# Output-projection halves inside the decode's closing chain, and running sums of squares on VectorE in two feed-forwards and the gate stage

## What is computed

```python
def rmsnorm(x, g):
    xf = x.astype(jnp.float32)
    y = xf * lax.rsqrt(jnp.mean(xf * xf, axis=-1, keepdims=True) + EPS)
    return (y * g.astype(jnp.float32)).astype(x.dtype)

def swiglu(x, w_gate, w_up, w_down):
    return (jax.nn.silu(x @ w_gate) * (x @ w_up)) @ w_down

x = x + FFN_RES * swiglu(rmsnorm(x, ffn_norm[layer, 0]), ...)   # ffn00, ffn10
# layer 0: s5_mixer, with   out = (y @ w_glu_v) * sigmoid(y @ w_glu_g)
# layer 1: mla_mixer, with  o = softmax(q . cache) . cache, mapped by w_uv;  return o @ w_o
x = x + FFN_RES * swiglu(rmsnorm(x, ffn_norm[layer, 1]), ...)   # ffn01, ffn11
```

## Time and profile before

| | us |
|---|---|
| median of 3 runs | 2287.75 |
| lowest and highest | 2266.84, 2288.28 |
| the profiled execution | 2266.89 |
| its span, first to last instruction | 2264.6 |
| closing chain, last scores ready to first projection matmul | 1785.27 to 1814.88 |

### The profile page before, as it was taken

The page is one execution under the profiler, slowest core; times in us unless marked ns, Lnnn a source line. Parts: engine busy times, 40 slices in busy tenths (PEclk is TensorE's granted clock), DMA queues, the critical chain, the costliest instruction groups (busy, mean ns, idle before and its releaser), DMA issues.

```text
span 2264.6 us, 46747 instructions
## 1 busy us (share of the span) xinstructions
PE 2127.8 (94%) x19825; PEld 2020.4 (89%) x19825; DVE 1087.0 (48%) x1563; ACT 745.5 (33%) x1080; POOL 157.2 (7%) x250
## 2 busy tenths in 40 slices
PE   7999999974899999999999999988888799999998
PEld 6999999953899999999999999975656599999998
DVE  5453676697344445322654442234763234544422
ACT  4222222543343343222422222242543124434211
POOL 3002010140000000000000000000027100000000
PEclk9999999997999999999999999999999799999999
DMA  6232323100222333332333333221237322333332
GB/s 134 84 107 71 93 85 107 39 3 6 85 84 85 93 93 88 103 90 63 95 92 93 93 101 90 79 80 29 50 105 203 88 66 78 90 93 93 105 90 77
DMA packets 355924, 192.56 MB, mean 85 GB/s; under 512 B 33005, under 2 KB 350443, under 8 KB 355795
## 3 DMA queue, kind: packets, MB, share of 16 engines
q1 hardware_dynamic: 348736, 180.19, 27.8%
q0 software_dynamic: 5488, 9.03, 1.4%
q10 hardware_dynamic: 1570, 1.48, 0.3%
HBM read 184.23 MB, written 3.02 MB: 83 GB/s over the span
## 4 chain that ended last, share of the span: by engine, by line
PE 85%; DVE 7%; ACT 3%; SPq 2%; issue 2%; DMA 1%; DVEq 0%; ACTq 0%
PE ps L1724 75%; PE ps L1737 2%; DVE stmp L466 2%; PE ps L2132 1%; PE ps L2257 1%; DVE xs L470 1%; PE ps L2288 1%; SPq L440 1%; SPq L438 1%; DVE stmp L469 1%; PE ps L2019 1%; PE ps L1743 1%; DVE wl L1126 1%; PE ps L2235 1%; DMA xin<-x_prompt 0%
## 5 line engine op out<-in xcount | busy, mean ns | idle before, releaser
L1724 PE MATMUL ps<-xh,wh 128*128 128x260 f32 x3296 | 870.1, 285 | 30.8 <-DVE xl L1441 15.8
L1724 PE MATMUL ps<-xl,wh 128*128 128x260 f32 x3296 | 863.6, 284 | 0.0
L1724 PE MATMUL ps<-xh,wl 128*128 128x260 f32 x3296 | 667.4, 284 | 0.0
L1724 PEld LDWEIGHTS ps<-xh,wh 128*128 128x128 f32 x3296 | 626.9, 190 | 37.7 <-issue 30.6
L1724 PEld LDWEIGHTS ps<-xl,wh 128*128 128x128 f32 x3296 | 625.0, 190 | 0.0
L1724 PEld LDWEIGHTS ps<-xh,wl 128*128 128x128 f32 x3296 | 512.1, 190 | 0.0
L650 ACT ACTIVATE wh<-raw 128x1024 fp32r<-128x1024 f32 (+1 forms) x150 | 175.6, 1170 | 597.7 <-PE ps L1724 596.5
L1126 DVE TENSOR_TENSOR wl<-raw,wh 128x1024 fp32r<-128x1024 f32 (+1 forms) x150 | 206.1, 1374 | 238.9 <-ACT wh L650 238.8
L1724 PE MATMUL ps<-hh,wh 128*128 128x260 f32 x1056 | 277.7, 284 | 0.0
L1724 PE MATMUL ps<-hl,wh 128*128 128x260 f32 x1056 | 275.6, 282 | 0.0
L668 ACT ACTIVATE wh<-raw 128x1024 fp32r<-128x1024 f32 (+1 forms) x124 | 135.3, 1091 | 418.3 <-PE ps L1724 418.3
(11 more groups left out here) (403 smaller groups left out, 2200.3 us busy)
## 6 DMA issues: line engine op xcount, KB each, us to landing
raw<-ffn_w_gate SPq DMA_DIRECT2D x88, 512.0 KB, 3.8
raw<-ffn_w_up SPq DMA_DIRECT2D x88, 512.0 KB, 3.8
raw<-ffn_w_down SPq DMA_DIRECT2D x64, 704.0 KB, 4.5
cb<-cache_ckv SPq DMA_DIRECT2D x72, 128.0 KB, 2.8
cb<-cache_ckv POOLq DMA_DIRECT2D x56, 128.0 KB, 2.9
raw<-s_w_glu_v SPq DMA_DIRECT2D x8, 512.0 KB, 3.8
raw<-s_w_glu_g SPq DMA_DIRECT2D x8, 512.0 KB, 3.7
raw<-mla_w_o SPq DMA_DIRECT2D x8, 512.0 KB, 4.1
```

What stands on the lines that cost most here:

```text
L1724: got = mm(ps[0:width, bank + half, 0:HALF], w[par_][:, k * width:k * width + width], src[:, k0 + k, half * HALF:half * HALF + HALF], star ...
```

## The change

First, the running sum. In ffn01, ffn10 and the gate stage VectorE adds the square of tile d-1 to the running sum in the other `sq` buffer (`add_squares`), from d = 2 on, and signals `ss_done` itself. TensorE sums only twice per stage: the running sum of tiles 0 to 6, and tile 7. The other stages keep their sums.

Second, the output projection. The first four tiles are made in halves of 24 matmuls (`wo_half`), the first 260 columns in banks 0 to 3, the others in banks 4 to 7. The first halves stand in the last iteration of the decode loop and between the steps of the closing chain. ScalarE and VectorE split two more weight blocks, WO0+2 and WO0+3, into extra buffers `w4h`, `w4l`, which lie where `cb0` was. The small results of the chain move to bank 7, two small VectorE steps (`own_w`, `own_s`) move to iteration 1 of the decode loop, and the turning of the maxima moves ahead of the last output. The update of x for these four tiles is two instructions.

```diff
+                w4h, w4l = take(m, ("w4h", [P, 2, KD * P], F32R), ("w4l", [P, 2, KD * P], F32R))
@@ ScalarE, decode loop
+                else:
+                    act.wait_ge(d_o, NB - 1)
+                    for j in range(2):
+                        act.wait_ge(w_in[(WO0 + j) % 2], slots.arrived(WO0 + 2 + j))
+                        run(w4h[:, j, :], raw[(WO0 + j) % 2][:, 0:KD * P], ACT.Copy).then_inc(w_hi, 1)
@@ ScalarE, projection
-                if d < KD - 1:
+                if d < 2:
+                    n = WO0 + 4 + d
+                    act.wait_ge(w_in[n % 2], slots.arrived(n))
+                    act.wait_ge(w_used, WO0 + d + 1)
+                    run(wh[n % 2][:, 0:KD * P], raw[n % 2][:, 0:KD * P], ACT.Copy).then_inc(w_hi, 1)
+                elif 4 <= d < KD - 1:
                     his(WO0 + d + 2)
@@ VectorE
+            def add_squares(tick):
+
+                now, before = tick % 2, (tick - 1) % 2
+                dve.wait_ge(sq_rdy, tick + 1)
+                tt(sq[:, now, :], sq[:, now, :], sq[:, before, :], ALU.add).then_inc(ss_done, 1)
@@ VectorE, ffn01 and ffn10
                     los(bd + 2 * d + 2)
+                    if name in NEXT and d >= 2:
+                        if d >= 3:
+                            dve.wait_ge(ss_done, SQ[name] + d - 2)
+                        add_squares(SQ[name] + d - 1)
                     update(d, bd + 2 * d + 1, d % 2)
@@ VectorE, gate stage
                 j = d % 2
+                if d >= 2:
+                    if d >= 3:
+                        dve.wait_ge(ss_done, SQ["glu"] + d - 2)
+                    add_squares(SQ["glu"] + d - 1)
                 if d < KD - 1:
                     los(g0 + 2 * d + 3)
@@ VectorE, decode loop and chain
+            def wide_lo(j):
+
+                dve.wait_ge(w_hi, WO0 + 3 + j)
+                tt(w4l[:, j, :], raw[(WO0 + j) % 2][:, 0:KD * P], w4h[:, j, :], ALU.subtract).then_inc(w_lo, 1)
+                else:
+                    wide_lo(0)
@@
-            copy(nwt[:, :, :], ps[:, 3, 0:NB * HP].rearrange("p (b h) -> p b h", b=NB))
             tt(wsel[:, :, :], cst[:, C_S32:C_S32 + HP].unsqueeze(1).to_broadcast([P, NB, HP]),
                ps[:, 4, 0:NB].unsqueeze(2).to_broadcast([P, NB, HP]), ALU.mult).then_inc(d_fin, 1)
+            own(copy(nwt[:, :, :], ps[:, 7, NB * HP:2 * NB * HP].rearrange("p (b h) -> p b h", b=NB)))
+            wide_lo(1)
@@ VectorE, projection
+                if d < 4:
+                    tt(x[:, d, 0:HALF], x[:, d, 0:HALF], ps[:, d, 0:HALF], ALU.add)
+                    tt(x[:, d, HALF:TOK], x[:, d, HALF:TOK], ps[:, d + 4, 0:HALF], ALU.add).then_inc(x_upd, 1)
@@ TensorE, ffn01 and ffn10, after the down-projection
+                if not each:
+                    pe.wait_ge(ss_done, S + KD - 2)
+                    sums(S + KD - 2, S % 2, True)
@@ TensorE, gate stage
                 product(g0 + 2 * d, g0 % 2, KD, X, 2 * (d % 2), ready=(xl_rdy, GEN["glu"]) if d == 0 else None)
+                if d == KD - 1:
+                    pe.wait_ge(ss_done, S + KD - 2)
+                    sums(S + KD - 2, S % 2, True)
                 if d >= 1:
-                    sums(S + d - 1, (S + d - 1) % 2, d == 1)
                     pe.wait_ge(g_sig, d)
                 product(g0 + 2 * d + 1, 1 - g0 % 2, KD, X, 5, free=d == KD - 1)
@@ TensorE, decode loop and chain
+            def wo_half(d, half, k0, k1):
+
+
+                pe.wait_ge(w_lo, WO0 + d + 1)
+                hi_, lo_ = (wh[(WO0 + d) % 2], wl[(WO0 + d) % 2]) if d < 2 else (w4h[:, d - 2], w4l[:, d - 2])
+                for k in range(k0, k1):
+                    for m, (w, srcs_) in enumerate(((hi_, (xh, xl)), (lo_, (xh,)))):
+                        for s, src in enumerate(srcs_):
+                            got = mm(ps[:, d + 4 * half, 0:HALF], w[:, k * P:k * P + P], src[:, k, half * HALF:half * HALF + HALF],
+                                     start=k == 0 and m == 0 and s == 0, stop=k == KD - 1 and m == 1)
+                if half == 1:
+                    got.then_inc(w_used, 1)
+                if b == NB - 1:
+                    pe.wait_ge(a_ol, NH // 2)
+                    wo_half(0, 0, 0, KD)
                 pe.wait_ge(d_e, b + 1)
@@
+                else:
+                    turn(ps[0:NB, 7, 0:P], mb[:, :])
+                    turn(ps[0:NB, 7, P:2 * P], lb[:, :]).then_inc(d_rt, 1)
+                    wo_half(1, 0, 0, 3)
@@ after the output of the last token
+            wo_half(1, 0, 3, KD)
+            wo_half(2, 0, 0, 3)
             pe.wait_ge(d_ws, 1)
...
+            wo_half(2, 0, 3, 5)
             pe.wait_ge(d_fin, 1)
...
+            wo_half(2, 0, 5, KD)
             pe.wait_ge(d_fin, 2)
...
+            wo_half(3, 0, 0, KD)
             pe.wait_ge(d_ol, 1)
             for d in range(KD):
-                if d >= 2:
+                if d < 4:
+                    wo_half(d, 1, 0, KD)
+                else:
                     pe.wait_ge(x_upd, UPD["wo"] + d - 1)
-                product(WO0 + d, (WO0 + d) % 2, KD, X, 2 * (d % 2), free=d == KD - 1)
+                    product(WO0 + d, (WO0 + d) % 2, KD, X, 2 * (d % 2), free=d == KD - 1)
```

More of the change, by code:

```diff
@@ L271, in yoco_step @@
                         ("mx", [P, 2, 4, 2], F32), ("nm", [P, 2, 4, 2], F32), ("sm", [P, 2, 4, 2], F32), ("rs", [P, 2, 4, 2], F32))
+            with ExitStack() as m:
+                w4h, w4l = take(m, ("w4h", [P, 2, KD * P], F32R), ("w4l", [P, 2, KD * P], F32R))
             with ExitStack() as m:
@@ L1650, in _ @@
                     turned(b + 1, 7)
-            dve.wait_ge(l_rdy, 1)
-            eye = ident[0:NB, 0:NB].unsqueeze(2).to_broadcast([NB, NB, HP])
-            own(tt(own_w[:, :, :], snew[:, :, :], eye, ALU.mult))
-            own(V.tensor_reduce(own_s[:, :], own_w[:, :, :].rearrange("p b h -> p h b"), AX.X, ALU.add))
+                if b == 1:
+                    dve.wait_ge(l_rdy, 1)
+                    eye = ident[0:NB, 0:NB].unsqueeze(2).to_broadcast([NB, NB, HP])
+                    own(tt(own_w[:, :, :], snew[:, :, :], eye, ALU.mult))
+                    own(V.tensor_reduce(own_s[:, :], own_w[:, :, :].rearrange("p b h -> p h b"), AX.X, ALU.add))
             dve.wait_ge(d_rt, 1)
-            copy(mrow[:, :, :], ps[0:NB, 0, 0:P].rearrange("p (q h) -> p q h", q=NQ))
-            own(copy(lrow[:, :, :], ps[0:NB, 1, 0:P].rearrange("p (q h) -> p q h", q=NQ)))
+            copy(mrow[:, :, :], ps[0:NB, 7, 0:P].rearrange("p (q h) -> p q h", q=NQ))
+            own(copy(lrow[:, :, :], ps[0:NB, 7, P:2 * P].rearrange("p (q h) -> p q h", q=NQ)))
             own(V.tensor_reduce(grow1[:, :], mrow[:, :, :].rearrange("p q h -> p h q"), AX.X, ALU.max))
@@ L1693, in _ @@
             for d in range(KD):
-                if d < KD - 1:
+                if d < 2:
+                    los(WO0 + d + 4)
+                elif 4 <= d < KD - 1:
                     los(WO0 + d + 2)
-                else:
+                elif d == KD - 1:
                     dve.wait_ge(x_upd, UPD["wo"] + d)
@@ L1700, in _ @@
                 dve.wait_ge(w_used, WO0 + d + 1)
-                tt(halves(x[:, d, :]), halves(x[:, d, :]), banks(2 * (d % 2)), ALU.add).then_inc(x_upd, 1)
+                if d < 4:
+                    tt(x[:, d, 0:HALF], x[:, d, 0:HALF], ps[:, d, 0:HALF], ALU.add)
+                    tt(x[:, d, HALF:TOK], x[:, d, HALF:TOK], ps[:, d + 4, 0:HALF], ALU.add).then_inc(x_upd, 1)
+                else:
+                    tt(halves(x[:, d, :]), halves(x[:, d, :]), banks(2 * (d % 2)), ALU.add).then_inc(x_upd, 1)
             dve.wait_ge(x_upd, UPD["wo"] + KD)
@@ L1840, in ffn @@
                 down(0, bd, 0)
-                down(1, bd + 2, 1, lambda: sums(S, S % 2, True))
+                each = name not in NEXT
+                down(1, bd + 2, 1, (lambda: sums(S, S % 2, True)) if each else None)
                 with pe.Fori(1, KD // 2) as i:
                     for j in range(2):
-                        down(i * 2 + j, i * 4 + (bd + 2 * j), j, lambda: sums(i * 2 + (S + j - 1), (S + j - 1) % 2, False))
+                        down(i * 2 + j, i * 4 + (bd + 2 * j), j,
+                             (lambda: sums(i * 2 + (S + j - 1), (S + j - 1) % 2, False)) if each else None)
+                if not each:
+                    pe.wait_ge(ss_done, S + KD - 2)
+                    sums(S + KD - 2, S % 2, True)
             def kv_sums():
@@ L2388, in _ @@
                 got.then_inc(d_o, 1)
-            pe.wait_ge(d_e, NB)
-            turn(ps[0:NB, 0, 0:P], mb[:, :])
-            turn(ps[0:NB, 1, 0:P], lb[:, :]).then_inc(d_rt, 1)
+            wo_half(1, 0, 3, KD)
+            wo_half(2, 0, 0, 3)
             pe.wait_ge(d_ws, 1)
-            mm(ps[:, 3, 0:NB * HP], ones[0:NB, :], own_w[:, :, :].rearrange("p b h -> p (b h)"), start=True, stop=True)
-            turn(ps[:, 4, 0:NB], mrow[:, :, :].rearrange("p q h -> p (q h)"), NB).then_inc(d_wp, 1)
```

(3 more changed lines are left out.)

8 lines of the change are left out of this document (4 added, 4 removed).

## The result

| | median of 12 runs | lowest to highest | profiled execution | span | mean granted clock |
|---|---|---|---|---|---|
| before | 2288.02 us | 2266.84 to 2291.83 | 2266.89 us | 2264.6 us | 0.969 |
| after | 2258.03 us | 2249.94 to 2265.42 | 2259.11 us | 2256.8 us | 0.963 |

The ratio of after to before is 0.9897, with a 95% interval from 0.9876 to 0.9919. The kernel is about 1.0% faster, right at the bound between "faster by over 1%" and "within 1%". The medians differ by more, 30.0 us, because 8 of the 12 runs before lie above 2284 us. One launch of a later kernel took 11617 us, for no reason that the record shows, and counts in none of the ratios.

The account below looks back on a forecast made before the run. TensorE, busy 94% of the span, was taken to bound the kernel. Terms 6.6 - 1.7 + 14.1 gave 19.0 us gained; the profile's ratio 0.9916, scaled to the median, gave 2268.6 us, range 2239 to 2277.

Parts of the forecast that it names:

- sums in ffn01 and ffn10: In the two feed-forwards, twelve inline sums dropped at 0.55 us each, replacing additions free: 6.6 us gained.
- gate stage: Six sums save 3.1 us, but a late addition idles TensorE 3.1 us and costs 1.7 of clock: 1.7 lost.
- closing chain and projection: End of decode attention: projection halves fill TensorE's waits, so product 4 starts 14.1 us earlier.
- Rival B: Gate stage: late addition does not idle TensorE or costs no clock; 2267 or 2264 us; chance 0.1.
- rival A: Closing chain: clock kept through L2401 and L2409; that part gains 19.9 us, total 2262.7; chance 0.2.
- L2401 warm, L2409 cold: Closing chain's two narrow matmul groups: first at full clock, 3.5 us; second at 1.2 GHz, 7.0 us.
- The first sum of the projection: Projection: it waits about 1.0 us for ScalarE's square, the second sum about 0.35 us.
- The two half updates: Projection: two 260-column updates of x take 0.76 us against 0.70 for one; first two sums wait 0.2 more in all.
- The levels: Whole kernel: runs before lie on two levels 21 us apart, profile on the lower, median on the upper.
- C: Closing chain: clock lost as before and halves run at 1.2 GHz; sum 10.5 us, 2277; chance 0.1.
- D: Closing chain: two extra weight blocks land late, delaying the chain; 2314 at 45 us late; 0.05 including overlooked causes.
- E: Whole kernel: runs after fall on the lower level, 2248 us, with before on the upper; chance perhaps 0.3.

Follow-up runs that it names:

- the part alone: The kernel before with the running sum of squares in the gate stage alone: ratio 1.0001, gate stage 111.97 us.
- Altering the order: Changed kernel with update and square of the projection's first two output blocks ahead of copy and split of weight blocks WO0+4 and WO0+5: ratio 0.99.
- the one profile with both at long values: Profile of the kernel before with the running sum of squares in the gate stage alone: 2287.88 us, ratio 1.0001.
- the first full weaving: Combined kernel (early addition, altered projection order, seven extra matmuls before S5), with wide block 3 matmuls among both narrow groups, all 24 kept: 2248.23 us, ratio 0.9865.
- the kernel with the old order: The kernel before with 81 extra matmuls, results unread, in the closing chain's gaps and nothing moved: ratio 0.9973, stretch 93.15 us.
- the second profile of the changed kernel: The changed kernel run once more, unaltered: ratio 0.9875, closing stretch 83.44 us.

## Why the prediction came out as it did

The touched stretches, as a mean over all profiles that have the old or the new code there, against the terms of the sum:

| term | predicted | first profile of after | mean over profiles |
|---|---|---|---|
| sums in ffn01 and ffn10 | -6.6 | -6.7 | -7.2 (5 without, 9 with) |
| gate stage | +1.7 | +0.65 | +1.9 (5 old, 4 with the late addition) |
| closing chain and projection | -14.1 | -17.9 | -13.2 (4 old, 4 new) |
| sum | -19.0 | -24.0 | -18.5 |

**Sums in the feed-forwards: right.** 0.55 us per sum was the right end of its range, and the additions cost nothing: each lies between a split and an update, as in the timeline above, at 0.69 us. Between profiles with the same clock lost the gain is 6.7 us, 0.56 per sum; the mean of 7.2 holds some luck with the clock.

**Gate stage: right in both its parts.** The addition ended 3.1 us after the product before it, and the product behind it was 1.7 us longer, in this kernel and with the part alone. Moving the one instruction gave 4.75 us back. Only the value of the old stage was off: 111.37 us in the profile I read, 110.25 to 110.63 in four others, since that profile had lost about 1 us more to the clock there. Rival B is out.

**Closing chain: mechanism right, one term mis-sized, and it is a term without a fixed size.** The output of token 7 took 1.86 us in place of 3.00. ScalarE's exponential (mrow) began at 1803.92, behind the copy of `ob` at 1803.64, as foreseen. The small matmuls took 0.54 for 0.6. The first narrow group took 3.50 for 3.5. The second was put at 7.0 and took 3.74. That the first profile gained 17.9 us where the forecast had 14.1 was luck with this one term. With the clock up until both groups were done, this is nearly rival A (19.9 us; measured 17.9). But in the three other profiles of the same code the first group took 4.4 to 5.1 us and the second 6.64. There the forecast's order of things holds, except that the fall came inside the first group. So "L2401 warm, L2409 cold" was a fair mean of outcomes that differ between executions, and the error was to treat it as one outcome. The first sum of the projection waited for 1.07 us, where the forecast had 1.0; the second hardly waited, where it had 0.35. Altering the order removed 1.1 us of idle time. Two slips in this part change nothing: the last addition comes to 14.6 us and not 14.5, and of the 3.00 us of token 7's old output not half but about 2.3 us ran at 1.2 GHz, since by the earlier trace rows the clock fell early in the window from 1789 to 1790.

**The two half updates.** In the chain of after, the first pair (L1739 and L1740) takes 0.43 and 0.34 us, 0.77 together, and the second pair 0.34 and 0.34. The forecast had 0.76 for a pair. By the estimate from the Trainium skill (VectorE: DVE Perf Modes, section on the TRN2 errata) it would be 0.86. For one instruction of 260 columns the same estimate gives 0.43 us, and the trace agrees with 0.42 to 0.43; it disagrees with adding two of them up, since the second half begins 0.34 us behind the first.

**The levels: a guess that was right in kind.** The forecast said that the runs before lie on two levels "which no row explains". They are now explained in part. The profile that I read, 2266.89 us, had both S5 (140.3) and the attention (300.5) at their shortest. The median of before, 2288, lies where the one profile with both at long values lies (2287.88); no execution of before at that level was itself profiled. The median of the first three runs, 2287.75, was in the upper set, and no run of after was as slow as the 2268.6 us scaled from it. The ratio was the sounder forecast: the mean of all 88 runs of before is 2281.1, of all 16 runs of the changed kernel 2257.6, a ratio of 0.9897. That is 23.5 us, against 18.5 from the ledger and 19.0 predicted. The remaining 4 to 5 us lie in how often each program meets the long values in code that the change doesn't touch, or in the small number of runs; I can't say which.

**Rivals C, D and E** did not come. E had the runs after at 2248; they spread from 2250 to 2265 around 2258. C would have needed the halves at 1.2 GHz. The clock was at 0.50 from 1784 to 1790, behind some 5 us without work, but it was back at 1.00 from 1792, and the first half took 3.07. D, the late weight blocks, did not come in the change, but the first full weaving met its small brother, a split that wasn't ready.

## What to carry to other kernels

Look for the instruction that gets queued behind a wait on the very engine that its reader is waiting for. The late addition was found by reading VectorE's order beside TensorE's chain, and moving that one instruction gave 4.8 us, where removing twelve groups of sums gave 6.7. Work moved into TensorE's gaps gave back the idle time in every profile (9 us here), while what it gives by the clock has to be counted over several profiles. Before believing a difference of 1% between two profiles, make a ledger by stage and look at the untouched stages first: here they moved by 17 us.

## What the runs showed of the hardware that I had not expected

- TensorE's clock fell from 2.4 to 1.2 GHz inside stretches that were busy throughout: the 64-matmul groups of S5 (1.83 us at one level, 3.51 at the other), and the narrow groups of the closing chain, with 39 dense matmuls shortly ahead in the kernel with the old order. Where it happens differs between executions of one program.
- Once fallen in narrow work, it stayed down while that lasted: in S5 the groups went on at 3.51 us, and around the narrow groups it was at 0.50 for 17 us in three profiles with the halves and for 20 us in the first full weaving. In dense work it rose again: in the second profile of the changed kernel the dense matmuls began at 1809.91 and the clock was back at about 1814.6.
- Transposes alone brought it back. In the kernel before TensorE did nothing but 128x128 f32 transposes from 1773.37 on, at 0.50, and from 1779 on the clock was 1.00; in the kernel after it was the same from 1785.28, with 0.50 until 1790, 0.80 in the next microsecond and 1.00 after it.
- With seven matmuls ahead of it whose results nothing reads, S5 began at 433.1 to 433.8 us instead of 431.0 to 432.7 and had its short value in all five profiles, 12.5 us below the long one. Whether the work or the delay did it is open. The Trainium skill, TensorE: Matmul & The Clock Gate, in its Part 1 on the clock gate, says that the first cold stretch of one kernel varies between executions, with the state of the clock gate at its start. The traces show such a variation too, but in the middle of a kernel and inside busy stretches. The page has the cost of the ramp at under 1% of a typical kernel; here two stages alone vary by 12.5 and 10.4 us of 2280, 1.0%, as much as the whole change is worth.
